# Moving 64 sample tokens of a product-key expert layer from dense TensorE products to gathered rows on VectorE

## The reference: what is computed

```python
q = (x @ w_q).reshape(n, PEER_HEADS, 2, PEER_HALF)
s = jnp.einsum('nhpd,hpkd->nhpk', q, sub_keys)
top_s, top_i = lax.top_k(s, PEER_TOPK)          # 16 of 128 keys on each side
cand_s = top_s[:, :, 0, :, None] + top_s[:, :, 1, None, :]
best_s, pos = lax.top_k(cand_s.reshape(n, PEER_HEADS, 256), PEER_TOPK)
idx = jnp.take_along_axis(cand_i, pos, axis=-1)  # 8 x 16 experts of a token
gate = jax.nn.softmax(best_s, axis=-1)
hid = gelu(einsum('td,thkd->thk', x, u_tab[idx]))
out = einsum('thk,thkd->td', hid * gate, v_tab[idx])
```

## Time and profile before

| | us |
|---|---|
| median of three executions | 5441.86 |
| profiled execution, first to last instruction (the span) | 5440.2 |
| PE busy | 5346.2 (98%) |
| DVE busy | 2340.7 (43%) |
| POOL busy | 2790.0 (51%) |
| ACT busy | 784.0 (14%) |
| query stage with its fillings | 1841 to 2243 |
| gate matrix stage | 2243 to 2543 |
| cover, values and steady steps | 2543 to 5413 |

### The profile page before, as it was taken

One profiled execution on the slowest core, in us unless ns is written; L12 is line 12 of the kernel. 1 busy time (PEld: TensorE's weight loads), 2 busy tenths in 40 slices (PEclk: granted clock), 3 DMA queues, 4 the chain that ended last, 5 costly groups with the idle time before them and its releaser, 6 DMA issues.

```text
span 5440.2 us, 97170 instructions
## 1 busy us (share of the span) xinstructions
PE 5346.2 (98%) x38870; PEld 5236.9 (96%) x38870; DVE 2340.7 (43%) x3887; ACT 784.0 (14%) x1693; POOL 2790.0 (51%) x1576
## 2 busy tenths in 40 slices
PE   7999999999999899999999999999999999999998
PEld 6999999999999899999999999999999999999997
DVE  7833342223421698486554333333333333333334
ACT  5520000111100100486000000000000000000001
POOL 4554444444555456433555555555555555555554
PEclk9999999999999999999999999999999999999999
DMA  3332222223343222356333222222222222222222
GB/s 111 99 112 77 76 81 82 95 95 119 120 160 105 82 84 94 130 165 211 139 129 111 100 93 95 99 95 93 101 95 99 94 94 100 94 91 102 94 91 93
DMA packets 232911, 571.51 MB, mean 105 GB/s; under 512 B 53904, under 2 KB 103312, under 8 KB 227472
## 3 DMA queue, kind: packets, MB, share of 16 engines
q1 hardware_dynamic: 232592, 566.54, 30.6%
HBM read 492.19 MB, written 74.28 MB: 104 GB/s over the span
## 4 chain that ended last, share of the span: by engine, by line
PE 97%; DVE 2%; issue 0%; ACT 0%; DMA 0%; POOL 0%; SPq 0%; DVEq 0%; ACTq 0%; POOLq 0%
PE ps L1685 90%; PE aux L2008 2%; PE aux L1841 2%; PE ps L1718 0%; PE aux L1969 0%; DVE nt L1058 0%; PE aux L1749 0%; PE aux L1909 0%; DVE rst L1076 0%; DVE oa L1526 0%; DVE mg L1058 0%; DVE xl L1064 0%; PE aux L1911 0%; DMA mg<-in_x 0%; PE aux L1935 0%
## 5 line engine op out<-in xcount | busy, mean ns | idle before, releaser
L627 POOL CAST wh<-wr 128x1024 fp32r<-128x1024 f32 x782 | 834.1, 1067 | 2536.5 <-PE ps L1685 1434.0
L629 POOL TENSOR_TENSOR wl<-wr,wh 128x1024 fp32r<-128x1024 f32 x782 | 1942.4, 2484 | 62.6
L1685 PE MATMUL ps<-xp,wh 128*128 128x288 f32 (+1 forms) x7552 | 1811.3, 323 | 0.0
L1685 PE MATMUL ps<-yp,wh 128*128 128x432 f32 (+1 forms) x6144 | 1611.7, 336 | 0.0
L1685 PE MATMUL ps<-xp,wl 128*128 128x288 f32 x4544 | 1327.7, 292 | 0.0
L1685 PEld LDWEIGHTS ps<-xp,wh 128*128 128x128 f32 x7552 | 1241.5, 188 | 18.9
L1685 PE MATMUL ps<-yp,wl 128*128 128x288 f32 x4096 | 1206.0, 294 | 0.0
L1685 PEld LDWEIGHTS ps<-yp,wh 128*128 128x128 f32 x6144 | 1040.6, 188 | 21.0
L1685 PE MATMUL ps<-xh,wh 128*128 128x288 f32 x3296 | 991.3, 301 | 1.6 <-DVE yt L1355 1.6
L1685 PE MATMUL ps<-xl,wh 128*128 128x288 f32 x3296 | 972.3, 295 | 0.0
L1685 PE MATMUL ps<-xh,wl 128*128 128x288 f32 x3296 | 968.9, 294 | 0.0
(11 more groups left out here) (269 smaller groups left out, 3802.0 us busy)
## 6 DMA issues: line engine op xcount, KB each, us to landing
wr<-in_w SPq DMA_DIRECT2D x786, 512.0 KB, 3.3
gates_s<-gbuf SPq DMA_DIRECT2D x12, 3072.0 KB, 11.9
gtile<-gates_s SPq DMA_DIRECT2D x32, 1152.0 KB, 6.3
gl<-hid_s SPq DMA_DIRECT2D x32, 288.0 KB, 3.7
hid_s<-gl SPq DMA_DIRECT2D x28, 288.0 KB, 4.5
qkv<-qkv_s SPq DMA_DIRECT2D x9, 768.0 KB, 5.6
mg<-in_x SPq DMA_DIRECT2D x4, 1152.0 KB, 12.6
qkv_s<-lo SPq DMA_DIRECT2D x16, 288.0 KB, 2.9
```

The costliest lines, as they stand in the source:

```text
L627: pool.tensor_copy(high[u][:, :, :], wr[u][:, :, :]).then_inc(S["hi_done"], 1)
L629: pool.tensor_tensor(low[u][:, :, :], wr[u][:, :, :], high[u][:, :, :].bitcast(F32), ALU.subtract).then_inc(S["lo_done"], 1)
L1685: mm_ = pe.matmul(two(out) if len(moving.shape) == 3 else out, weights[w][:, t, :], moving, start=first and t == tiles_[0] and not more, s ...
```

## The change

The 64 sample tokens leave the dense PEER products. All hidden and value products now have TD = 512 columns, one whole bank, in three matmuls per weight tile (`dense`). The queries keep 576 tokens (`whole`). With one bank per product, each slot alternates between its two banks (`k // 2`, `d % 2`), and TensorE waits for the product before the one before in that slot (`- 1` in the waits on `evacuated`). VectorE and ScalarE work in place in PSUM: gelu, the gate multiplication and the low part have PSUM operands in the steady steps. `fold` and the second addition are gone.

```diff
-        def joined(p):
+        def dense(p, low_at, half=0):
             def passes(k):
-                yield wh, 0, p[:, k, 0:PH], 0, 0
-                yield wl, 0, p[:, k, 0:HT], 1, 1
-                yield wh, 1, p[:, k, PH:2 * PH], 0, 0
-                yield wh, 1, p[:, k, 2 * PH:2 * T], 1, 0
-                yield wl, 1, p[:, k, PH:PH + HT], 1, 1
+                yield wh, half, p[:, k, 0:TD], 0, 0
+                yield wh, half, p[:, k, low_at:low_at + TD], 1, 0
+                yield wl, half, p[:, k, 0:TD], 1, 1
...
-        def added(g, j, x):
-            dve.tensor_tensor(halves(mg[:, j, :]), halves(mg[:, j, :]), both(x), ALU.add).then_inc(S["summed"], 1)
-            wait("summed", KD * g + j + 1)
-            dve.tensor_tensor(two(mg[:, j, 0:HT]), two(mg[:, j, 0:HT]), ps[x][:, :, HT:PH], ALU.add
+        def added(d, x):
+            j = 2 * d + x
+            dve.tensor_tensor(mg[:, j, 0:TD], mg[:, j, 0:TD], bank(x, d % 2), ALU.add
                               ).then_inc(S[f"evacuated{x}"], 1)
```

For the sample tokens each of 64 steps handles two picks of all 64 tokens, one per half of the partitions (128 = 64 tokens x 2 copies). GpSimd gathers one row of 2048 values per partition (1 MB per step) by indirect DMA from the untransposed tables, two row buffers alternating:

```diff
+SP_N = H * TOPK // SP_COPIES
+STEADY = 8 * (EARLY - 1)
+DOT_AT = [s + 5 for s in range(SP_N)]
+SUM_AT = [STEADY + 16 * (s // G2) + 2 * (s % G2) + 1 for s in range(SP_N)]
+GATHER_AT = [1, 3] + [a + 3 for a in STEP_AT[:-ROWS]]
...
+        def gather(s):
...
+            else:
+                pool.wait_ge(S["row_done"], s - ROWS + 1)
+            j = s % SP_N
+            pool.indirect_dma_start(out=rows[r_][:, :], out_offset=None, in_=u_in if s < SP_N else v_in,
+                                    in_offset=bass.IndirectOffsetOnAxis(ap=expert[:, j:j + 1], axis=0)
+                                    ).then_inc(S[f"row_in{r_}"], 16)
...
+        def dot(s):
...
+            dve.scalar_tensor_tensor(rows[r_][:, :], rows[r_][:, :], 1.0, wide_aux, ALU.mult, ALU.mult,
+                                     accum_out=hid[:, s:s + 1]).then_inc(S["row_done"], 1)
+        def row_sum(s):
...
+            dve.scalar_tensor_tensor(wide_aux, rows[r_][:, :], hid[:, s - SP_N:s - SP_N + 1], wide_aux,
+                                     ALU.mult, ALU.add).then_inc(S["row_done"], 1)
```

GpSimd's gathers stand between its splits, three slots after the step whose buffer they refill. SyncE's waits change too, because the gate multiplication now works in place in `gl`:

```diff
         def hidden_load(g, k):
             if g or k >= 2:
-                sp.wait_ge(S["m_done"], G2 * g + k - 1)
+                sp.wait_ge(S["m_lo"], G2 * g + k - 1)
```

More of the change, by code:

```diff
@@ L239, in trunk_program @@
     gsum = r.take("gsum", [128, NBL * H])
[L240 to L252, removed]
+    spare = at["CV"] + 4 * CONST["upper"][0]
+    r = Region(spare, at["CV"] + 4 * CONST["iota16"][0])
+    expert = r.take("expert", [128, SP_N], U32)
+    weight = r.take("weight", [128, SP_N])
+    hid = r.take("hid", [128, SP_N])
     ps = [nc.alloc_psum_tensor(f"ps{i}", [128, 2, 512], F32) for i in range(2)]
@@ L965, in _, with high @@
         gmats(NTB // 2 - 1, True)
[L968 to L981, removed]
+        def high(n, source):
+            act.wait_ge(S["m_done"], n + 1)
+            act.activation(yp[:, n % (2 * G2), 0:TD], source, ACT.Copy).then_inc(S["m_hi"], 1)
         def cover(k):
@@ L1621, in _ @@
-        wait("gt_in0", 16)
-        for k in range(G2):
-            wait(f"gl_in{k % 2}", 16 * (k // 2 + 1))
-            gated(0, 0, k)
-            gated_low(0, 0, k)
-        for g in range(EARLY - 1):
-            collect(HPV + 4 * g, g, kept_low(g + 1), kept_high(g + 1))
-        with loop(dve, 0, (NG - EARLY) // 2 - 1) as i:
-            for u in range(2):
-                hidden(HPS + 8 * (2 * i + u), EARLY + 2 * i + u, i, u)
-                collect(HPS + 8 * (2 * i + u) + G2, EARLY - 1 + 2 * i + u, last_low(EARLY + 2 * i + u, u),
-                        last_high(EARLY + 2 * i + u, u))
@@ new lines, in _, with after @@
+        kept_gated(0, 0)
+        kept_low(0, 0)
+        kept_gated(0, 1)
+        kept_low(0, 1)
+        wait("weighed", TD // 4)
+        x_wide()
+        kept_gated(0, 2)
+        kept_low(0, 2)
+        kept_gated(0, 3)
+        kept_low(0, 3)
+        for g in range(EARLY - 1):
+            def after(d):
+                if d % 2 == 0:
+                    kept_gated(g + 1, d // 2)
+                sparse(8 * g + d)
+            collect(HPV + 4 * g, g, lambda d: kept_low(g + 1, d // 2) if d % 2 else None, after)
@@ new lines, in _ @@
+        for g in range(EARLY - 1, NG - 1):
+            at_ = STEADY + 16 * (g + 1 - EARLY)
+            for k in range(G2):
+                sparse(at_ + 2 * k)
+                gated(g + 1, k)
+                sparse(at_ + 2 * k + 1)
+                if k < G2 - 1:
+                    low(g + 1, k)
+            collect(HPS + 8 * (g + 1 - EARLY) + G2, g, lambda d: low(g + 1, G2 - 1) if d == 0 else None,
+                    lambda d: sparse(at_ + 8 + d))
+        wait("sums_added", SP_COPIES)
@@ L1683, in piece @@
                 for weights, half, moving, more, final in passes(k0 + t - tiles_[0]):
-                    out = ps[slot][:, half, 0:int(np.prod(moving.shape[1:]))]
-                    mm_ = pe.matmul(two(out) if len(moving.shape) == 3 else out, weights[w][:, t, :], moving,
+                    mm_ = pe.matmul(ps[slot][:, half, 0:moving.shape[1]], weights[w][:, t, :], moving,
                                     start=first and t == tiles_[0] and not more,
@@ L2038, in _ @@
         for g in range(EARLY - 1):
-            values(HPV + 4 * g, g, g % 2, [e + g * KD // 2 for e in EV_V])
-        def step(g, hp, par):
+            values(HPV + 4 * g, g, [e + g * KD // 2 for e in EV_V], 8 * g)
+        for g in range(EARLY - 1, NG - 1):
             base = [e + PER_G * (g - EARLY + 1) for e in EV_S]
-            hidden(hp, base[0], base[1])
-            values(hp + G2, g, par, [e + G2 // 2 for e in base])
-        with loop(pe, 0, (NG - EARLY) // 2) as i:
-            for u in range(2):
-                step(EARLY - 1 + 2 * i + u, HPS + 8 * (2 * i + u), 1 - u)
```

373 lines of the change are left out of this document (231 added, 142 removed).

## The result

Four executions of the changed kernel took 5055.80 to 5062.53 us, median **5059.17**; the kernel before took 5442.05 in the same comparison. The ratio is 0.9297 (95% interval 0.9283 to 0.9310): 7.0% faster. Forecast were 5047 us and a range of 4975 to 5125. The profiled execution took 5062.53 us with a span of 5060.7.

A forecast was written before the change was run, and what follows sets the result against it. TensorE, busy 98% of the span, was taken as the bound. From 5440.2 us, -411.3 (dense), -13.0 and -16 (gate), +3.5 and +1.5 (transposes, wait), +40 (early pieces) gave 5044.9, median 5047; range 4975 to 5125.

The forecast's parts named there:

- The 512-column matmul: Dense products on TensorE: 229.0 ns per matmul, 687 ns per tile of three, so -411.3 us (bounds -453 and -403).
- rival C: Matmul excess belongs to weight loads and vanishes at 512 columns: about 216 ns each, 4887 us; chance 0.03.
- The gate stage: Gate matrix: 16 units fewer, -13.0 us; TensorE's waits and handovers halved, -16 us (bounds 0 and -31).
- Query stage: Query products: TensorE arrives 7.9 us earlier at the turn, still after VectorE's search; no change in time.
- Transposes and their wait: After the gate stage: 32 more transposes, +3.5 us; the first 16 wait for `staged`, +1.5 us (0 to 4).
- The early pieces: First value pieces, with dots and gathers: VectorE, GpSimd and DMA nearly full, +40 us (bounds 0 and +221).
- The step that made 40: Early pieces: DMA at 289 GB/s costs +55, and loads queue behind `hidden_load`'s wait for the low part; together +40 us.
- rival B: Early pieces: gathers slow to issue or land, GpSimd's split late, slot 7.5 us, +128: 5135 us; chance 0.15.
- A: Early pieces lose nothing, as the cover of VectorE, GpSimd and DMA holds: 5007 us; chance 0.20.
- D: Gathers not spread over DMA engines, 48 us each: slower than before, some 8700 us; chance 0.03.

The follow-up runs named there:

- e3: Changed kernel with the same dots and sums spread, one at every third piece: 5022.13 us.
- e1: Changed kernel with the sample tokens' whole path (gathers, dots, sums, transposes) left out: 5017.45 us.
- e2: Changed kernel with the next group's first kept hidden part loaded one piece earlier: 5025.24 us.
- e8: Changed kernel with dots of 64 elements instead of 2048, all gathers and waits kept: 5034.73 us.
- e5: On e3: yp, the moving operand of the value products, starts 128 bytes later: 4980.54 us.
- e9: Changed kernel with yp starting 128 bytes later and nothing else: 5023.14 us.
- e10: On e5: every SBUF tensor 384 bytes later, distances between them kept: 4980.56 us, one run.
- e11: On e3: yp starts 256 bytes later instead of 128: 5022.54 us, one run.
- e4: Changed kernel with rows of yp 4224 instead of 4096 bytes apart: 5051.84 us.
- e6: On e3: a 128-byte gap between yp's high and low parts, pitch 4224 bytes: 5004.82 us, one run.

## Why the prediction was right, and where it was off

The order of the terms holds; they are compared here one by one.

**The 512-column matmul.** Taken at 229.0 ns, bounds 225.6 and 229.7. Measured: 226.7 for hidden products, inside and near the lower bound, and 233.3 for values, outside. The extension of two shapes by a line assumed one operand like another. The tiles so cost 6144 x (226.7 + 233.3) ns = 2826 us instead of 2814: the term is -399, not -411.3. The mean of the two, 230.0, was off by only 1.0 because the errors cancel in part: that is luck. The rule of the Trainium skill, TensorE: Matmul & The Clock Gate (Wait — 56ns, not 53.3ns?), 215.8 ns at 512 columns, is 11 ns under the best that any run here showed; the prediction's rival C falls.

**The gate stage.** It ran from 2259.5 to 2552.7 us, 293.2; products take 16 x 10.88 = 174 and units 128 x 0.81 = 104, so 15 are left, as taken; 294.6 was forecast. But they are not waits:

```profile
2259.50:2549.00 289.50, 288.86 (x1768) 255.42 (x1768) 226.11 (x251) 230.73 (x650) 119.65 (x64) 1.00 0.61 181
```

TensorE stands for 0.6 us here, where it stood for 12.9 before. The six product matmuls between two units take 1.47 us (2550.47 to 2551.94 us) instead of 6 x 226.7 ns = 1.36, which makes 14 us in 128 units. "I halve the waits" gave the right number; in fact the standing went nearly whole and the handovers stayed.

**Query stage.** The turn came at 2171.1, forecast 2170.0, without a wait for VectorE. The stage, taken at nothing, came out 2 us too long: 1841.2 to 2259.5 us is 16.6 more than 1841.3 to 2243.0, and the products account for 14.4 (20 x 10.88 against 16 x 12.70).

**Transposes and their wait.** Two sets of 16, 1.7 us each to the start of the next product, forecast 3.5 together; TensorE waited 0.8 us for the first, forecast 1.5. `x_wide` took 4.48 us, not 2.3, beside a subtraction of GpSimd:

```profile
2582.64 2.72 POOL L653 TENSOR_TENSOR wl<-wr,wh 128x1024 fp32r<-128x1024 f32 x1
2583.02 4.48 DVE L1647 TENSOR_TENSOR rows<-xp 128x2048 f32<-128x2048 f32 x1
```

The dots have as many elements and took 2273 to 2290 ns, all 64 of them, beside the same work of GpSimd. They have one operand in PSUM, `x_wide` has two in SBUF. The Trainium skill, SBUF — State Buffer (SBUF: two separate sides), says that VectorE with two SBUF inputs and GpSimd exclude each other at a shared port pair; the trace agrees, as `x_wide` ended 2.1 us after the subtraction that had begun before it, about the length of a dot. All of it together: e3 less e1, 4.7 us, against 5.0.

**The early pieces.** Forecast +40 between 0 and 221; measured 5059.2 - 5022.1 = 37 by e3, 34 by e2. Of the inputs, a gather's issue was 0.97 to 0.99 us (taken 1.5), its landing 7.4 (taken 7.6), a dot 2.28. With these the loop of two buffers takes (2.28 + 0.98 + 7.4) / 2 = 5.3 us a slot and by itself costs nothing beside pieces of 5.60. The step that made 40 went by two things, a DMA limit and SyncE's queue. The DMA limit is not it: e2 moves more bytes per us without loss. The queue is, but with another load than I had named: I had SyncE held by its new wait on the low part, with the gate load and a weight load behind it, and TensorE in want of that low part. What was late was the kept part at the head of a group, and the delay went VectorE, dot, `row_done`, gather, split. I had named GpSimd's late split only for rival B. Whether the new wait on `m_lo` adds to the lateness was not tried: in the rows above the two parts were issued straight behind the weight load. The half clock after each stand, 11 us, was in no term. So the place of the loss was right and half of its grounds; that 40 came so near to 37 is luck.

**Sum.** From the profiled execution before: 5440.2 - 399 - 13 - 16 + 3.4 + 0.8 + 37 = 5053. The profiled execution, 5060.7, was the slowest of four; the median of 5059.2 stands for a span of 5057.4. Of the 4 us in between the query stage has 2; the rest was not followed up. Of the prediction's rivals, A (no loss) is e3's schedule, not this one; B would have needed 12.7 us from dot to row, measured about 8.4; D falls with a landing of 7.4 us for 1 MB.

## What to carry to other kernels

A wait is as dear as what is queued behind it. In e1 kept parts were late by 2.3 us each and it cost TensorE nothing; in e8 they were nearly as late as in the changed kernel and TensorE stood for 8 us in all; with a dot of 2.3 us, a gather and a split behind each it stood for 27, and the lower clock after each stand took some 11 more. When one engine's pieces shrink, look for loads that were just in time and issue them a piece earlier, and spread optional work over all pieces instead of packing it where the others are fullest. And try an operand at other offsets before comparing shapes: here a shift of 128 bytes was worth 36 to 42 us.

## What the runs showed that was not expected

An fp32r matmul of 512 columns took 226.7 ns when its moving operand lay 0 bytes (yp in e5, e9, e10) or 256 bytes (the low part of xp) from the offset of the weights modulo 512, 237 and 229 by turns when 128 bytes off either way (the changed kernel, e11), and 228 to 235 with rows 4224 bytes apart (e4), 234 and 226 by turns with a gap of 128 bytes between the parts as well (e6). In the kernel before, no difference between the two operands was to be seen with 288 and 432 columns. A gather of 128 rows of 8 KB held GpSimd for 0.97 to 0.99 us and landed in 7.4 us beside 290 GB/s of traffic; 64 of them in 390 us brought the core to 298 GB/s, and 319 in e2.
